# The last down projection of a two-block transformer kernel, turned from column tiles to token tiles

## What is computed

```python
def conv_ffn(x, norm_g, w_gate, w_up, conv_w, conv_b, w_down):
    h = rmsnorm_2(x, norm_g)
    gate = causal_dwconv(h @ w_gate, conv_w) + conv_b
    return (jax.nn.silu(gate) * (h @ w_up)) @ w_down      # 5632 -> 2048

def second_block(...):
    ...
        x = x + conv_ffn(x, ffn_norm_g[l], w_gate[l], w_up[l], ffn_conv_w[l], ffn_conv_b[l], w_down[l])
    return rmsnorm_2(x, final_norm_g)                     # mean of squares over the 2048 channels
```

## Time and profile before

| | us |
|---|---|
| median of 3 runs | 2573.48 (2572.52 to 2575.47) |
| the profiled execution, as a whole | 2573.6 |
| its span, first to last instruction | 2571.8 |
| down_2 on PE, first matmul to last | 2305.8 to 2556.9 |
| last eviction, norm and stores | 2556.95 to 2571.8 |

### The profile page before, as it was taken

One profiled execution on the slowest core, in us unless ns is written; L12 is line 12 of the kernel. 1 busy time (PEld: TensorE's weight loads), 2 busy tenths in 40 slices (PEclk: granted clock), 3 DMA queues, 4 the chain that ended last, 5 costly groups with the idle time before them and its releaser, 6 DMA issues.

```text
span 2571.8 us, 37914 instructions
## 1 busy us (share of the span) xinstructions
PE 2491.5 (97%) x14958; PEld 2207.5 (86%) x14958; DVE 1647.3 (64%) x2157; ACT 1254.7 (49%) x1620; POOL 65.0 (3%) x61
## 2 busy tenths in 40 slices
PE   8989898999999999988999999999999999999998
PEld 7878797888888888877889989888888888888886
DVE  6898757656566554547776446866767676765454
ACT  5555555444444443445454345654544444454343
POOL 0000000000000000000003210000000000000000
PEclk9999899999999999999999999999999999999999
DMA  7553254565556555554553335554555555555553
GB/s 244 188 140 114 66 164 139 188 190 185 192 184 195 181 195 169 196 175 143 189 178 99 99 123 181 164 180 148 180 182 194 182 194 184 191 188 188 180 182 129
DMA packets 238146, 436.27 MB, mean 170 GB/s; under 512 B 18568, under 2 KB 34968, under 8 KB 237904
## 3 DMA queue, kind: packets, MB, share of 16 engines
q1 hardware_dynamic: 234496, 423.66, 51.0%
q0 software_dynamic: 2240, 6.80, 0.8%
q10 hardware_dynamic: 1296, 4.19, 0.4%
HBM read 432.51 MB, written 3.69 MB: 170 GB/s over the span
## 4 chain that ended last, share of the span: by engine, by line
PE 86%; DVE 9%; ACT 3%; issue 1%; DMA 1%; DVEq 0%; SPq 0%; ACTq 0%
PE ps L829 46%; PE ps L832 23%; PE ps L838 3%; PE ps L840 3%; PE ps L841 3%; DVE w_lo L455 3%; DVE ar L1277 2%; ACT w_hi L449 1%; PE ps L2280 1%; PE ps L2286 1%; PE ps L815 1%; PE ps L817 1%; PE ps L818 1%; DVE x L970 1%; PE ps L1310 0%
## 5 line engine op out<-in xcount | busy, mean ns | idle before, releaser
L455 DVE TENSOR_TENSOR w_lo<-w_raw,w_hi 128x1024 fp32r<-128x1024 f32 (+3 forms) x820 | 994.3, 1218 | 762.7 <-ACT w_hi L449 761.4
L449 ACT ACTIVATE w_hi<-w_raw 128x1024 fp32r<-128x1024 f32 (+3 forms) x820 | 853.6, 1046 | 906.0 <-PE ps L832 783.1
L829 PE MATMUL ps<-x,w_hi 128*128 128x512 f32 x3936 | 1244.2, 398 | 35.4 <-issue 15.0
L832 PEld LDWEIGHTS ps<-x,w_lo 128*128 128x128 f32 x3936 | 743.0, 189 | 176.1
L832 PE MATMUL ps<-x,w_lo 128*128 128x256 f32 x3936 | 776.3, 279 | 0.0
L829 PEld LDWEIGHTS ps<-x,w_hi 128*128 128x128 f32 x3936 | 603.1, 190 | 38.1 <-issue 26.1
L829 PE MATMUL ps<-h,w_hi 128*128 128x512 f32 x1408 | 444.1, 397 | 4.6 <-DVE w_lo L455 4.6
L832 PEld LDWEIGHTS ps<-h,w_lo 128*128 128x128 f32 x1408 | 265.3, 188 | 62.8
L832 PE MATMUL ps<-h,w_lo 128*128 128x256 f32 x1408 | 277.3, 278 | 0.0
L838 PE MATMUL ps<-x,w_hi 128*128 128x256 f32 x768 | 224.4, 292 | 1.5 <-DVE w_lo L455 1.1
L829 PEld LDWEIGHTS ps<-h,w_hi 128*128 128x128 f32 x1408 | 215.1, 189 | 5.6 <-DVE w_lo L455 5.5
(11 more groups left out here) (341 smaller groups left out, 1690.7 us busy)
## 6 DMA issues: line engine op xcount, KB each, us to landing
w_raw<-in_w_gate SPq DMA_DIRECT2D x88, 1024.0 KB, 5.1
w_raw<-in_w_up SPq DMA_DIRECT2D x88, 1024.0 KB, 5.1
w_raw<-in_w_down SPq DMA_DIRECT2D x88, 1024.0 KB, 5.1
w_raw<-in_w_in SPq DMA_DIRECT2D x79, 1024.0 KB, 5.1
w_raw<-in_w_out SPq DMA_DIRECT2D x32, 1024.0 KB, 5.1
w_raw<-in_w_xkv SPq DMA_DIRECT2D x8, 1024.0 KB, 5.0
w_raw<-in_w_uq SPq DMA_DIRECT2D x18, 256.0 KB, 3.8
w_raw<-in_w_ukv SPq DMA_DIRECT2D x16, 256.0 KB, 3.8
```

Source lines behind the costliest of these rows:

```text
L449: nc.scalar.activation(w_hi[:, u % HIS, 0:ks.stop - ks.start, cs], w_raw[:, slot(g, j), ks, cs], ACT.Copy)\
L455: nc.vector.tensor_tensor(w_lo[:, slot(g, j), ks, cs], w_raw[:, slot(g, j), ks, cs], w_hi[:, u % HIS, 0:ks.stop - ks.start, cs].bitcast(F3 ...
L829: nc.tensor.matmul(bank, w_h(k, cs), x(k).rearrange("p a n -> p (a n)"), start=(n == 0 and k == 0), stop=False)
L832: ins = nc.tensor.matmul(bank[:, T:2 * T], w_l(k, cs), x(k)[:, 0, :], start=False, stop=(final and k == ks.stop - 1))
```

## The change

`down_2` becomes one turn of four groups of 512 columns in the swap form, with the new kind "fin"; its loop on SP, DVE and ACT is written out. Results now have tokens on the partitions. The residual is brought into that layout by 32 transposes of 128x128 on PE, four ahead of each of units 4 to 11 (`fin_turn_pe`), into banks 4 to 7; ACT copies them out between its weight splits (`fin_keep_act`). DVE adds a finished group to it straight from PSUM and later multiplies by the gain, which now lies along the free dimension and is loaded once as a row spread over the partitions, 1 MB on POOL's queue (`fin_evict_dve`). ACT squares and sums along the free dimension (`fin_evict_act`), so the sums on PE go and the root works on 128x2. The last scaling is shared by DVE (5 pieces of 128x512) and ACT (3), and SP issues eight stores of 256 KB (`fin_store`) in token layout.

```diff
-            Gemm("down_2", 2, [group(w_loop(A["w_down_2"], 0, 1024), 11, out=(xt, 0, 8), kind="add"),
-                               group(w_loop(A["w_down_2"], 512, 1024), 11, out=(xt, 4, 8), kind="add")], h2c),
+            Gemm("down_2", 1, [group(w_cols(A["w_down_2"], W * q, W), 11, kind="fin", banks=2 * (q % 2)) for q in range(4)], h2c),
...
-                gr["form"] = "swap" if gr["kind"] == "v" else g.form
+                gr["form"] = "swap" if gr["kind"] in ("v", "fin") else g.form
...
+                    if u in before and first_turn(i):
+                        before[u]()
...
-        STREAM_STAT = {"w_out": "mix", "down": "ff", "down_2": "final"}
+        STREAM_STAT = {"w_out": "mix", "down": "ff"}
...
+        def fin_turn_pe(pe, p):
+            if p == 0:
+                pe.wait_ge(evicted, G["down_2"].e0)
+            if p >= 4:
+                pe.wait_ge(fin_kept, p - 3)
+            for m in range(4):
+                last = nc.tensor.transpose(fin_bank(p)[:, m * P:(m + 1) * P], xt[:, p // 2 * 4 + m, p % 2 * P:(p % 2 + 1) * P], ident[:])
+            last.then_inc(fin_turned, 1)
+
+        def fin_keep_act(act):
+            for p in range(4 * TT):
+                yield
+                act.wait_ge(fin_turned, p + 1)
+                nc.scalar.activation(fin_x[:, p // 2, p % 2, :], fin_bank(p), ACT.Copy).then_inc(fin_kept, 1)
+
+        def fin_evict_act(act, g, gr):
+            for t in range(TT):
+                n = TT * gr["n"] + t
+                act.wait_ge(evicted, g.e0 + n + 1)
+                if n >= TT:
+                    act.wait_ge(fin_sq, n - 1)
+                nc.scalar.activation(half[:, 2 * t:2 * t + 2, :].rearrange("p c t -> p (c t)"), fin_x[:, gr["n"], t, :],
+                                     ACT.Square, accum_out=fin_ssq[:, t, gr["n"]:gr["n"] + 1]).then_inc(fin_sq, 1)
+
+        def fin_evict_dve(dve, g, gr):
...
+            for t in range(TT):
+                group_ready(dve, g, 0, gr, t)
+                dve.wait_ge(fin_kept, TT * q + t + 1)
+                x = fin_x[:, q, t, :]
+                nc.vector.tensor_tensor(x, x, ps[:, gr["banks"] + t, :], ALU.add).then_inc(evicted, 1)
+                if last:
+                    dve.wait_ge(evicted, g.e0 + TT * q + t + 1)
+                    gear(t)
+            if last:
+                dve.wait_ge(fin_sq, 4 * TT)
+                nc.vector.tensor_reduce(fin_total, fin_ssq, AX.X, ALU.add).then_inc(st_sum, 1)
+                return
+            yield
+            yield
+            dve.wait_ge(fin_gain_in, 16)
+            for t in range(TT):
+                dve.wait_ge(fin_sq, TT * q + t + 1)
+                gear(t)
...
+        FIN_ORDER = [(0, 0), (1, 0), (0, 1), (0, 2), (1, 1), (0, 3), (1, 3), (1, 2)]
+
+        def fin_scale_dve(dve):
+            dve.wait_ge(fin_geared, 4 * TT)
+            for t, q in FIN_ORDER:
+                if fin_mine(t, q):
+                    y = fin_piece(t, q)
+                    nc.vector.tensor_scalar(y, y, st_y[:, t:t + 1], None, ALU.mult).then_inc(fin_dve, 1)
...
+        def fin_store(sp):
+            done = {True: 0, False: 0}
+            for t, q in FIN_ORDER:
+                mine = fin_mine(t, q)
+                done[mine] += 1
+                sp.wait_ge(fin_dve if mine else fin_act, done[mine])
+                sp.dma_start(out[:, t, q * W:(q + 1) * W], fin_piece(t, q)).then_inc(out_done, 16)
+            sp.wait_ge(out_done, 16 * len(FIN_ORDER))
...
+            pool.wait_ge(products, AHEAD_P + G["down_2"].p0)
+            pool.dma_start(fin_gain, A["final_row"].partition_broadcast(P).rearrange("a b n -> a (b n)")).then_inc(fin_gain_in, 16)
...
-            run_("down_2")
-            g = G["down_2"]
-            finish(evict_act(act, g, g.turns - 1, g.groups[-1]))
+            run_("down_2", fin_keep_act(act))
+            fin_evict_act(act, G["down_2"], G["down_2"].groups[-1])
             root(act, "final")
-            for k in range(4):
-                act.wait_ge(out_ready, k + 1)
-                act.dma_start(out[:, 4 * k:4 * k + 4, :], tx[:, 4 * k:4 * k + 4, :]).then_inc(out_done, 16)
-            act.wait_ge(out_done, 64)
+            fin_scale_act(act)
...
-            multiply(pe, G["down_2"])
+            def residual(p):
+                return lambda: fin_turn_pe(pe, p)
+
+            multiply(pe, G["down_2"], before={4 + p: residual(p) for p in range(4 * TT)})
```

More of the change, by code:

```diff
@@ L487, in evict_act @@
                 return
+            if gr["kind"] == "fin":
+                yield
+                fin_evict_act(act, g, gr)
+                return
             if gr["form"] == "wide":
@@ L570, in evict_dve @@
                     reduce_group(dve, g, i, gr)
+                return
+            if gr["kind"] == "fin":
+                yield from fin_evict_dve(dve, g, gr)
                 return
@@ L783, in run, with multiply @@
                     turn(eng, split, evict, g, i, evict(eng, g, i - 1, g.groups[-1]))
-        def multiply(pe, g, *stats, between=None, filler=None, at=FIRST + 1):
+        def multiply(pe, g, *stats, between=None, filler=None, at=FIRST + 1, before={}):
             def body(i, first=0, last=g.units):
@@ new lines, in build, with fin_bank @@
+        fin_total = st_v[:, 40:40 + TT]
+        fin_turned, fin_kept, fin_sq, fin_geared = sem("fin_turned"), sem("fin_kept"), sem("fin_sq"), sem("fin_geared")
+        fin_gain_in, fin_dve, fin_act = sem("fin_gain_in"), sem("fin_dve"), sem("fin_act")
+        def fin_bank(p):
+            return ps[:, 4 + p % 4, :]
+        def fin_turn_pe(pe, p):
[6 more added lines that the diff above has]
+            last.then_inc(fin_turned, 1)
@@ new lines, in fin_evict_dve, with gear @@
+        def fin_evict_dve(dve, g, gr):
+            q, last = gr["n"], gr is g.groups[-1]
+            gain = fin_gain[:, q * W:(q + 1) * W]
+            def gear(t):
+                x = fin_x[:, q, t, :]
+                nc.vector.tensor_tensor(fin_tail[:, t, :] if last else x, x, gain, ALU.mult).then_inc(fin_geared, 1)
+            for t in range(TT):
+                group_ready(dve, g, 0, gr, t)
+                dve.wait_ge(fin_kept, TT * q + t + 1)
+                x = fin_x[:, q, t, :]
+                nc.vector.tensor_tensor(x, x, ps[:, gr["banks"] + t, :], ALU.add).then_inc(evicted, 1)
[5 more added lines that the diff above has]
+                nc.vector.tensor_reduce(fin_total, fin_ssq, AX.X, ALU.add).then_inc(st_sum, 1)
+                return
+            yield
+            yield
+            dve.wait_ge(fin_gain_in, 16)
+            for t in range(TT):
+                dve.wait_ge(fin_sq, TT * q + t + 1)
+                gear(t)
@@ new lines, in fin_piece, with fin_mine @@
+        def fin_piece(t, q):
+            return fin_tail[:, t, :] if q == 3 else fin_x[:, q, t, :]
+        def fin_mine(t, q):
+            return t == 0 or q == 3
+        FIN_ORDER = [(0, 0), (1, 0), (0, 1), (0, 2), (1, 1), (0, 3), (1, 3), (1, 2)]
[5 more added lines that the diff above has]
+                    nc.vector.tensor_scalar(y, y, st_y[:, t:t + 1], None, ALU.mult).then_inc(fin_dve, 1)
@@ new lines, in fin_scale_act @@
+        def fin_scale_act(act):
+            act.wait_ge(st_done, STATS["final"][0] + 1)
+            act.wait_ge(fin_geared, 4 * TT)
+            for t, q in FIN_ORDER:
+                if not fin_mine(t, q):
+                    y = fin_piece(t, q)
+                    nc.scalar.activation(y, y, ACT.Copy, scale=st_y[:, t:t + 1]).then_inc(fin_act, 1)
+        def fin_store(sp):
+            done = {True: 0, False: 0}
+            for t, q in FIN_ORDER:
+                mine = fin_mine(t, q)
[3 more added lines that the diff above has]
+            sp.wait_ge(out_done, 16 * len(FIN_ORDER))
@@ L1135, in variance_dve @@
             dve.wait_ge(st_sum, STATS[name][0] + 1)
-            nc.vector.tensor_scalar(var_of(name)[0], sum_out(name), 1.0 / norm(name)[0], EPS, ALU.mult, ALU.add)\
+            nc.vector.tensor_scalar(var_of(name)[0], fin_total if name == "final" else sum_out(name), 1.0 / norm(name)[0], EPS, ALU.mult, ALU.add)\
                 .then_inc(st_var, 1)
@@ L2476, in _ @@
                 load(sp, g)
+            fin_store(sp)
         @block.gpsimd
@@ L2798, in _ @@
             run_("down_2")
-            g = G["down_2"]
-            finish(evict_dve(dve, g, g.turns - 1, g.groups[-1]))
+            finish(fin_evict_dve(dve, G["down_2"], G["down_2"].groups[-1]))
             refine(dve, "final")
[L2802 to L2805, removed]
+            fin_scale_dve(dve)
         @block.tensor
@@ L2892 @@
            for n, v in arrays.items()}
-    out = nc.dram_tensor("out_t", [P, DC, T], F32, kind="ExternalOutput").ap()
+    out = nc.dram_tensor("out_t", [P, TT, D], F32, kind="ExternalOutput").ap()
     build(nc, aps, out)
```

23 lines of the change are left out of this document (14 added, 9 removed).

## The result

| | before | after |
|---|---|---|
| median | 2572.68 us (2567.84 to 2575.47, 5 runs) | 2559.99 us (2557.28 to 2563.01, 5 runs) |
| after / before | | 0.995, 95% interval 0.9936 to 0.9963 |
| profiled execution: whole / span | 2573.6 / 2571.8 us | 2557.84 / 2556.0 us |
| stage down_2, first to last matmul with one spacing | 250.96 us | 243.25 us |
| last result E to the end of the span | 14.85 us | 10.75 us |

The medians are 12.7 us apart, and the forecast was 11.5. A second measurement of both kernels gives 2561.42 us (2559.85 to 2562.97, 5 runs) against 2573.07 (9 runs), ratio 0.9954 (0.994 to 0.9967), 11.65 us.

What follows compares the result with a forecast made beforehand. TensorE, busy 97% of the span, was taken to bound the kernel, with a tail ended by store bandwidth. Stage -7.3 and tail -4.2 gave -11.5 us, from the 2573.48 median to 2562 us, range 2558.5 to 2568.5.

Steps and rivals of the forecast that it cites:

- The pace of a unit: In down_2, 12 matmuls of 512 columns take 2.722 us a unit instead of 2.787, gaining 5.7 us over 88 units.
- the rival in which the old pace stays: Units of down_2 stay at 2.787 us, so 5.7 us are missing and the time is 2567.7 us; chance 0.08.
- The loop: One turn in down_2 keeps the loads' lead of 4 tiles, removing two gaps and the half clock: 4.4 us gained.
- The sum matmuls: The six fp32 matmuls on TensorE that add up the norm's squares in down_2 go: 1.3 us gained.
- The transposes: 32 added on TensorE, four ahead of each of units 4 to 11, cost 4.1 us, bounds 3.3 and 4.9.
- The added waits: In down_2, weights behind ScalarE's copies are ready after 3.3 us and needed at 6.5: 3.2 us to spare, cost 0.
- The tail: From last result E to the span's end, stores end by bandwidth: E + 10.6 us against 14.85, gaining 4.2.
- The rival in which they lose half of their rate: The final eight 256 KB stores run at half of 410 GB/s, 5.1 us longer: 2567.1 us; chance 0.05.
- The slower rival: ScalarE's wait for transposes makes weights late, stopping TensorE at eight units, 3.6 us each: 28 us, 2590 us; chance 0.04.
- a shift of another stage by more than 2 us: A sign that the forecast is wrong: a stage other than the changed one moves by more than 2 us.

Runs made afterwards that it cites:

- the short lead alone: The one-turn wide kernel with the loads of tiles 22 and 23 made to wait for tiles 20 and 21: 2572.38 us, stage 250.70 us.
- the first experiment: The kernel before with down_2 in one turn of four groups, still wide, old tail: 2567.19 us against 2573.59, stage 246.53 us.
- the third experiment: The changed kernel without its 32 transposes, ScalarE copying the residual as it lies: 2556.38 us, stage 239.40 us.
- the run with two queues: The changed kernel with ScalarE issuing the three stores it scales and SyncE the other five: 2563.92 us.

## Why the prediction was right

It was right in its sum and in nearly all of its terms. The stage fell by 7.7 us where 7.3 had been forecast, and the tail by 4.1 where it was 4.2.

**The pace of a unit.** Taken as 2.722 us from 48 matmuls of another stage. Over the whole stage without transposes it is 2.7205, so the rival in which the old pace stays is out.

**The loop.** Taken as 4.4 us, from reading two gaps and a stretch of slow clock out of the trace. One turn alone gives 250.96 - 246.53 = 4.4 us, and the short lead alone takes 4.2 of it back. The total and its cause were right. Its division into 1.95 and 0.8 for the gaps and 1.6 for the half clock says where the time went, and not what each would give back: with the short lead the clock stays at 1.00, and other stops take the place of the 1.6.

**The sum matmuls.** 1.3 us, not measured alone, but the stage of the first experiment less 88 units at the old pace leaves 1.3. With the pace they make the 7.1 us between the first and the third experiment, where the prediction has 7.0.

**The transposes.** Taken as 4.1 us, measured 3.85 by leaving them out. A unit with them was to take 3.24 and takes 3.21. Left out, taken once and taken twice, they cost 0.11 us for each added one and a small rest for the switch; read this way, the prediction's 0.10 for each return was too much by about 0.04.

**The added waits.** Taken at nothing, with 3.2 us to spare. Moving the turns one unit later, which takes a unit away from that, leaves one stop of 0.28 us in the whole stage; two units later, every turn stops TensorE. So the spare time was there, and it was of the size given. The gain's load, 1 MB on GpSimd's queue, landed after 7.4 us and delayed no weights.

**The tail.** Taken as E + 10.6, measured 10.75. Two terms moved against each other: the first store came at E + 3.45 where 3.6 was expected, and the stores moved 385 GB/s where 410 was taken from the larger stores of before, so the 2.1 MB took about 5.5 us instead of 5.2. SyncE's issues of up to 0.65 us were hardly ahead of the 0.68 us that 256 KB take at 385 GB/s; that the bytes set the end all the same is shown by the run with two queues. The rival in which they lose half of their rate is out. The Trainium skill, "DMA: Bandwidth & Descriptors", section "Bandwidth", asks for 1 MiB and more in a transfer; eight stores of 256 KB reach 385 GB/s here without it. The prediction's reason, that several are in flight, was argued from the trace and not tested.

**The slower rival.** Its mechanism was right: moved two units, the turn makes the kernel slower in just that way. Its price was too low. It took 3.6 us a stop, the stop at 2428 in the trace of before with its slow clock; the stops measured cost 5.0 each, 2.89 of standing instead of 1.95 and about 2.1 of slow clock instead of 1.6.

**The other 4 us of the profiled pair.** The prediction named a shift of another stage by more than 2 us as a sign against it. down_2 starts at 2305.78 before and at 2301.80 after, with no engine's work changed ahead of it. Some 1.4 us of this are there already at the first matmul of `down` (897.98 and 896.55); the granted clock differs ahead of it too (0.80 and 0.90 on the mean of 280 to 300, 0.83 and 0.91 of 310 to 330). 0.6 us are lost again at a stop for weights that takes 3.01 us before and 3.57 after. The rest comes with two more stretches in which the clock differs. They stand here for before, for after, and for the changed kernel measured again:

```profile
1340.00:1350.00 10.00, 8.42 (x56) 7.78 (x56) 8.13 (x14) 3.97 (x5) 0.00 (x0) 0.83 0.62 224
1620.00:1630.00 10.00, 7.18 (x33) 6.05 (x32) 8.93 (x18) 9.61 (x19) 0.00 (x0) 0.83 0.36 118
```
```profile
1340.00:1350.00 10.00, 8.41 (x68) 7.86 (x67) 9.48 (x16) 4.60 (x5) 0.00 (x0) 1.00 0.54 193
1620.00:1630.00 10.00, 7.18 (x42) 6.09 (x41) 9.51 (x17) 10.00 (x18) 0.00 (x0) 1.00 0.33 107
```
```profile
1340.00:1350.00 10.00, 8.42 (x58) 8.06 (x57) 8.72 (x15) 3.86 (x5) 0.00 (x0) 0.83 0.70 250
1620.00:1630.00 10.00, 7.18 (x34) 6.06 (x33) 8.92 (x18) 8.93 (x17) 0.00 (x0) 0.83 0.45 149
```

Before, the clock fell at both places (0.83 on the mean of 10 us). After, in the profiled execution, it fell at neither; the work behind each starts earlier by a further 1.5 us. In the same changed kernel measured again it falls at both places as before did, and down_2 starts at 2304.56. That is still 1.2 us ahead of 2305.78: at a third place, 1780 to 1790, the clock is 0.83 before and 1.00 in this execution. So this part differs between executions of one kernel and is not the change's. The spread of the five runs of the changed kernel, 5.7 us, fits it: the two shortest have a mean clock of 0.992, the two longest 0.990. Why the clock falls at the same pause in one execution and not in another is open.

## What to carry to other kernels

A ring of buffers keeps its full lead over a loop only when the number of tiles in a turn suits the number of buffers: with 22 tiles over 4 the lead fell to two tiles at the second turn and cost 2.9 and 4.4 us in the two stages that do this. The first block's gate and up projections, 11 turns of 8 tiles over the same 4 buffers, show no such hole: from 440 to 890 us of the kernel before TensorE is busy for all of the 450 us, and SyncE's longest wait ahead of a load is 5.2 us. So look for a hole between two loads in the queue's timeline, well ahead of the stop on the engine that it causes. Where a busy engine sets the pace, count what the new form adds to its own stream (32 transposes, 3.85 us) against what it takes away (sum matmuls, pace and gaps, 11.5 us), and check how many us a hand-over through another engine has to spare: here it was 3.2, about one unit. And compare a profiled pair from the first changed instruction on, since the part ahead of it can differ by itself by a third of the gain.

## What had not been expected of the hardware

The same stop of 1.8 us was followed by the 1.2 GHz level before and by no fall of the clock in the run with the short lead, and both stages took 251 us. In the second the splits, which had lost their lead, stopped TensorE three times instead of twice, so a spell of slow clock cost next to nothing where late weights were the bound. In the run with the transposes two units later it did cost, about 2.1 us a stop. The stores with rows of 2 KB moved 382 GB/s on the mean of 4 us with the DMA engines full, from one queue and from two, where the loads with rows of that size had reached 408 in 3 us and the larger stores of before 406 on the mean of 4 us; whether the length of the rows makes the difference was not tried. While they ran, issuing a store took SyncE up to 0.65 us, against 0.36 for the first, and up to 1.19 with ScalarE issuing too.
